# A one-core decoder block: operands of the second feed-forward and of the mixer moved by 128 bytes, and one operand laid out in two regions

## The chip, the cores and the metric

The kernel runs on one core of one Trainium2 chip, as one program. The metric is the device time in microseconds, the median of several runs.

## The reference

The reference is one layer of a decoder block on 256 tokens with 2048 features, preceded by 16 learned tokens (272 rows in all). Everything is float32.

```
hs = concat(meta, x)                                             # 272 x 2048
hs = hs + 0.5 * swiglu(rmsnorm(hs), ffn1_w_gate, ffn1_w_up, ffn1_w_down)   # width 5632
hs = hs + token_mixing(rmsnorm(hs), w_in, ..., w_out)            # two causal convolutions, 3 and 31 taps
hs = hs + 0.5 * swiglu(rmsnorm(hs), ffn2_w_gate, ffn2_w_up, ffn2_w_down)
return rmsnorm(hs)[:, 16:]
```

with `swiglu(h) = (silu(h @ w_gate) * (h @ w_up)) @ w_down`. The weights are read from memory once, 339 MB in all.

## The kernel before, in words

All products are done on TensorE in a split form. Each float32 operand is split into a high part (a rounded copy, `w_hi`, `x_hi`, `a_hi`, `y_hi`, written by ScalarE) and a low part (the difference, `w_lo` and so on, written by VectorE), and a product is the sum of three matmuls: high by high, high by low, low by high. Every matmul has a 128 x 128 stationary operand, which a weight load (LDWEIGHTS, the rows of PEld) puts into the array, and a moving operand that is streamed past it. The load for the next matmul is issued while the current one streams.

The phases follow one another on TensorE in this order: gu1 and down1 (first feed-forward), ag, cv and b (the input projection of the mixer), out_sc and out_cf (its output projection), gu2 and down2 (second feed-forward). Weights come in blocks of 128 x 1024 (512 KB) through a ring of four buffers: a DMA on the SP queue fills `raw`, ScalarE writes `w_hi` from it (L650), VectorE writes `w_lo` (L886), TensorE uses both. ScalarE waits for TensorE to be done with a block four back before it overwrites it.

In gu1, down1, ag, cv, b, out_sc and out_cf the weights are stationary and the activations are moving: 272, 260 or 256 columns, three matmuls a product (`product`, L466 high by high, L467 weight high by activation low, L468 weight low by activation high). In gu2 the weights are stationary too, but high and low activations are streamed in one matmul of 512 columns (`wide_product`, L473), and the third product is a second matmul of 256 columns (L474). In down2 (`last_group`) the roles are swapped: the activations `a2_both` are stationary and the weights are the moving operand, 512 columns (L567, L568, L569).

Where the operands lie is written by hand. The numbers are bytes within a partition. The ring buffers start at a multiple of 512 and each block is 4096 bytes, so a stationary tile of weights (128 columns, 512 bytes) and a moving piece of weights (512 columns, 2048 bytes) start at a multiple of 512. The regions `x_at` and `a_at` start at a multiple of 512 as well. From there, all taken modulo 256:

- gu1 and ag: row tile k of `x_hi` (1088 bytes each) starts at 64 k, that of `x_lo` 64 further.
- down1: `a_hi` at 64 k, `a_lo` 128 further. cv: `x_hi` at 64 k + 48. b: `x_hi` at 64 k + 64.
- out_sc and out_cf: `y_hi` and `y_lo` (1024 bytes a tile, the two parts 16384 bytes apart) all start at 64, since `mix_at` is `a_at + 64`.
- gu2: `x2_both` (2048 bytes a row tile, high part then low part without a gap) always starts at 0.
- down2: the stationary tiles of `a2_both` (512 bytes) start at 0.

`gu2_lo` is a staging buffer that ScalarE fills from PSUM at the end of each gu2 group. `y_f`, `cs`, `zc`, `z`, `zd`, `tap_product` and the `ln_` rows are the mixer's working buffers behind `y_both`; they are placed relative to `mix_at` and are read and written by ScalarE and VectorE.

Of the kernel before, what the change touches and what calls it, by code (L numbers as in the profile page):

```python
# [29 lines left out]
F32R = mybir.dt.float32r  # L30

P = 128
# [4 lines left out]
SET = 4  # L37


def build(nc, x, meta_tokens, ffn1_norm, ffn1_w_gate, ffn1_w_up, ffn1_w_down, mix_norm, w_in, b_in,  # L40
# [3 lines left out]
    SEQ = x.shape[1]  # L44
    META = meta_tokens.shape[0]
    T = META + SEQ
    FF = ffn1_w_gate.shape[2]
    KD = D // P
    KF = FF // P
# [31 lines left out]
    with ExitStack() as ctx:  # L81
# [11 lines left out]
        x_at = nc.sbuf_base  # L93
# [6 lines left out]
        a_at = nc.sbuf_base  # L100
# [18 lines left out]
        def at(name, offset, shape, dt=F32):  # L119
            return nc.alloc_sbuf_tensor_at(name, shape, dt, offset=offset)  # L120

        x_hi = at("x_hi", x_at, [P, KD, T], F32R)
        x_lo = at("x_lo", x_at + 4 * (KD * T + X_GAP), [P, KD, T], F32R)
        x2_both = at("x2_both", x_at, [P, KD, 2, SEQ], F32R)

        o_tok = at("o_tok", x_at, [P, HALVES, D])
        gain_tok = at("gain_tok", x_at + 4 * HALVES * D, [P, D])
        sq_tok = at("sq_tok", x_at + 4 * (HALVES + 1) * D, [P, HALVES, BANK])
        a1_hi = at("a_hi", a_at, [P, KF, T], F32R)
        a1_lo = at("a_lo", a_at + 4 * (KF * T + A_GAP), [P, KF, T], F32R)  # L130
        a2_both = at("a2_both", a_at, [P, 2, KF, SEQ], F32R)
        a_of = {"gu1": (a1_hi, a1_lo),
                "gu2": (a2_both[:, 0, :, :], a2_both[:, 1, :, :])}

        gu2_lo = at("gu2_lo", a_at + 4 * 2 * KF * SEQ, [P, SET, SEQ])
        assert SET * SEQ <= 2 * KF * (T - SEQ)

        x_tok = at("x_tok", a_at, [P, HALVES, D])
        m_rows = at("m_rows", a_at + 4 * HALVES * D, [P, HALVES, P])
# [1 line left out]
        gain_rows = at("gain_rows", a_at + 4 * (HALVES + 1) * D + 16 * P, [KD, P])  # L141

        tile_bytes = 4 * SEQ
        mix_at = a_at + 64
        y_both = at("y_both", mix_at, [P, 2, 2 * KS, SEQ], F32R)
        y_hi, y_lo = y_both[:, 0, :, :], y_both[:, 1, :, :]
        y_f = at("y_f", mix_at + 4 * KS * tile_bytes, [P, KS, SEQ])
# [25 lines left out]
        def param(name, i):  # L173
            if name == "ffn1":
                return gain1[:, i:i + 1]
            return par[:, 0, row0[name] + i:row0[name] + i + 1]
# [55 lines left out]
        def slot(phase, g, i):  # L232
            return (n_blocks[phase] * g + i) % RING if isinstance(g, int) else i % RING
# [7 lines left out]
        def banks_before(phase, g):  # L241

            return KD + SET * group0[phase] + SET * g
# [20 lines left out]
        def over_groups(engine, phase, body):  # L264

            n = n_groups[phase]
            body(0, 0)
            if n > SET:  # L270
                with engine.Fori(1, n - 1, 2) as g:
                    body(g, 1)
                    body(g + 1, 0)
            else:
                for g in range(1, n - 1):
                    body(g, g % 2)
            if n > 1:
                body(n - 1, 1)
# [5 lines left out]
        def tokens(phase):  # L284

            return slice(T - width[phase], T)
# [131 lines left out]
        def _(pe):  # L418
# [13 lines left out]
            def start_between(i):  # L432

                if i in (0, 1, 3):
                    for q in {0: (2, 3), 1: (4, 5), 3: (6, 7)}[i]:
                        turn_pair(q)
                if i == 5:
                    pe.wait_ge(par_loaded, 16 * (len(rows0) + 4))
                    pe.wait_ge(emptied, KD)
                    for s in range(4):  # L440
                        pe.transpose(ps[:, 4, s * P:s * P + n_rows[s]], par_rows[0:n_rows[s], s, :],
                                     ident[0:n_rows[s], 0:n_rows[s]]).then_inc(par_turned, 1)
# [20 lines left out]
            def product(bank, n, w_high, w_low, act_high, act_low, first, last):  # L463

                dst = ps[:, bank, 0:n]
                pe.matmul(dst, w_high, act_high, start=first, stop=False)  # L466
                pe.matmul(dst, w_high, act_low, start=False, stop=False)  # L467
                return pe.matmul(dst, w_low, act_high, start=False, stop=last)  # L468

            def wide_product(bank, w_high, w_low, act_both, act_high, first, last):  # L470

                wide = ps[:, bank, :].rearrange("p (b t) -> p b t", b=2)
                pe.matmul(wide, w_high, act_both, start=first, stop=False)  # L473
                return pe.matmul(ps[:, bank, 0:SEQ], w_low, act_high, start=False, stop=last)  # L474

            def start_group(phase, g):

                if phase != "gu1" or not isinstance(g, int) or g > 0:
                    pe.wait_ge(emptied, banks_before(phase, g) - SET)

            def start_block(phase, g, i):

                pe.wait_ge(lo_ready, before_block(phase, g, i) + 1)

            def square_sums(norm, phase):

                pe.wait_ge(sum_ready[norm], 5 if norm == "start" else KD)
                pe.matmul(ps[:, 7, 0:width[phase]], ones[:, :], sq_sum[:, tokens(phase)],
                          start=True, stop=True).then_inc(stats_done[norm], 1)

            def paired(phase, norm):
                toks = tokens(phase)

                def body(g, parity):
                    first_group = isinstance(g, int) and g == 0
                    start_group(phase, g)
                    if norm and isinstance(g, int) and g == 1:
                        pe.wait_ge(var_ready[norm], 1)
                        if norm == "start":
                            pe.wait_ge(par_ready, 4)  # L500
                    for i in range(n_blocks[phase]):
                        s = slot(phase, g, i)
                        opening = norm == "start" and first_group
                        if opening and i == 0:
                            pe.wait_ge(first_lo, 1)
                        else:
                            start_block(phase, g, i)

                        for j, c in ([(j, c) for c in range(4) for j in range(2)] if opening
                                     else [(j, c) for j in range(2) for c in range(4)]):  # L510
                                k = 4 * (i // 2) + c
                                if norm and first_group and i % 2 == 0 and j == 0:
                                    pe.wait_ge(xlo_ready[norm], k + 1)
                                if opening and i == 0 and c == 2 and j == 0:
                                    start_block(phase, g, i)
                                cols = slice(c * 256 + j * P, c * 256 + (j + 1) * P)
                                bank = SET * parity + 2 * (i % 2) + j
                                if phase == "gu2":
                                    m = wide_product(bank, w_hi[s][:, cols], w_lo[s][:, cols],
                                                     x2_both[:, k, :, :], x2_both[:, k, 0, :],  # L520
                                                     k == 0, k == KD - 1)
                                else:
                                    m = product(bank, width[phase], w_hi[s][:, cols], w_lo[s][:, cols],
                                                x_hi[:, k, toks], x_lo[:, k, toks], k == 0, k == KD - 1)
                        m.then_inc(block_used, 1)
                        if norm and first_group and i == (6 if norm == "start" else 3):
                            square_sums(norm, phase)
                        if norm == "start" and first_group:
                            start_between(i)
                over_groups(pe, phase, body)  # L530

            def single_group(phase, g, parity, high, low, first_k, toks, n_k, ready, per_block, extra=None):
# [108 lines left out]
        def _(act):  # L641
# [10 lines left out]
            def operand(phase, norm, t):  # L652

                toks = tokens(phase)

                act.wait_ge(emptied, 2 * (t // 2) + 2 if norm == "start" else banks_before(norm, 0) + t + 1)
                dst = x2_both[:, t, 0, :] if phase == "gu2" else x_hi[:, t, toks]
                act.activation(dst, res[:, t, toks], ACT.Copy,
                               scale=param(gain_of[norm], t)).then_inc(xhi_ready[norm], 1)

# [219 lines left out]
        def _(dve):  # L880
# [8 lines left out]
            def operand(phase, norm, t):  # L889

                toks = tokens(phase)
                dve.wait_ge(xhi_ready[norm], t + 1)
                high, low_part = ((x2_both[:, t, b, :] if phase == "gu2" else (x_hi, x_lo)[b][:, t, toks])
                                  for b in (0, 1))
                dve.scalar_tensor_tensor(low_part, res[:, t, toks], param(gain_of[norm], t),  # L895
                                         high.bitcast(F32), ALU.mult,
                                         ALU.subtract).then_inc(xlo_ready[norm], 1)
# [350 lines left out]
```

## Time and profile before

| | us |
|---|---|
| median of 3 runs | 1882.8 (1873.69, 1882.8, 1882.98) |
| the profiled execution | 1873.64 |
| its span, first to last instruction | 1871.8 |
| TensorE busy | 1859.9 (99%) |
| TensorE weight loads busy | 1758.7 (94%) |
| VectorE busy | 1112.3 (59%) |
| ScalarE busy | 922.3 (49%) |
| mean granted TensorE clock | 0.999 of full speed |

The time lies 1.8 us over the span. A matmul's duration runs from its start to the modelled end of its results, so successive matmuls overlap in the records; how fast TensorE works is read from the distance between the starts of two matmuls. In a stretch of the window view, the count in brackets holds the matmuls that overlap the stretch, so the two or so that began before it are counted too.

### The profile page before, as it was taken

The numbers are of one execution on the slowest core, as the hardware profiler recorded it, in microseconds if no ns is written. First come the engines' busy times: TensorE is split into PE (matmuls) and PEld (weight loads), VectorE is DVE, ScalarE is ACT, GpSimd is POOL, SyncE is SP. The second block draws the span as 40 slices with busy tenths as digits, with TensorE's granted clock in tenths as the row PEclk, the third lists the DMA queues.
The fourth block names the chain that finished last, engine by engine and source line by source line (L and its number), as shares of the span: only waits on it lengthen the run. The fifth ranks groups of instructions, "written<-read, shape, count | busy, mean of one in ns | idle before, by whom it ended". The sixth has DMA issues, their size and how long they took to land.

```text
span 1871.8 us, 32101 instructions
## 1 busy us (share of the span) xinstructions
PE 1859.9 (99%) x13017; PEld 1758.7 (94%) x13017; DVE 1112.3 (59%) x1218; ACT 922.3 (49%) x1173; POOL 5.9 (0%) x17
## 2 busy tenths in 40 slices
PE   9999999999999999999999999999999999999998
PEld 9999999999999999999999999888888888888886
DVE  7555555555554545468899887555566655544444
ACT  6434333343343444359888665444444444443443
POOL 1000000000000000000000000000000000000000
PEclk9999999999999999999999999999999999999999
DMA  6655555555555555555666566666656666666664
GB/s 222 192 178 173 175 178 170 178 174 173 179 172 178 176 175 178 176 174 170 187 185 178 173 201 186 189 189 189 190 179 188 191 192 193 210 193 190 193 190 134
DMA packets 283357, 342.26 MB, mean 183 GB/s; under 512 B 10639, under 2 KB 223985, under 8 KB 283152
## 3 DMA queue, kind: packets, MB, share of 16 engines
q1 hardware_dynamic: 282672, 340.44, 58.6%
q8 instruction: 57, 0.93, 0.2%
q10 hardware_dynamic: 320, 0.53, 0.1%
q14 instruction: 20, 0.16, 0.0%
q0 software_dynamic: 288, 0.19, 0.0%
HBM read 339.02 MB, written 2.10 MB: 182 GB/s over the span
## 4 chain that ended last, share of the span: by engine, by line
PE 98%; DVE 1%; DMA 0%; ACT 0%; SPq 0%; issue 0%; DVEq 0%
PE ps L466 20%; PE ps L467 20%; PE ps L468 20%; PE ps L473 17%; PE ps L474 9%; PE ps L568 4%; PE ps L567 4%; PE ps L569 4%; DMA x_tok<-in_x 0%; DVE w_lo L886 0%; PE ps L428 0%; PE ps L585 0%; DVE zc L1098 0%; PE ps L591 0%; DVE ln_mu L912 0%; SPq L323 0%
## 5 line engine op out<-in xcount | busy, mean ns | idle before, releaser
L886 DVE TENSOR_TENSOR w_lo<-raw,w_hi 128x1024 fp32r<-128x1024 f32 x639 | 781.7, 1224 | 652.5 <-ACT w_hi L650 647.4
L650 ACT ACTIVATE w_hi<-raw 128x1024 fp32r<-128x1024 f32 x639 | 675.5, 1058 | 845.6 <-PE ps L468 505.6
L466 PE MATMUL ps<-x_hi,w_hi 128*128 128x272 f32 (+2 forms) x2048 | 588.1, 287 | 1.2 <-DVE x_lo L895 1.2
L467 PE MATMUL ps<-x_lo,w_hi 128*128 128x272 f32 (+2 forms) x2048 | 587.3, 287 | 0.0
L468 PE MATMUL ps<-x_hi,w_lo 128*128 128x272 f32 (+2 forms) x2048 | 583.4, 285 | 0.0
L473 PE MATMUL ps<-x_both,w_hi 128*128 128x512 f32 x1408 | 488.4, 391 | 0.0
L474 PE MATMUL ps<-x_both,w_lo 128*128 128x256 f32 x1408 | 394.1, 280 | 0.0
L467 PEld LDWEIGHTS ps<-x_lo,w_hi 128*128 128x128 f32 x2048 | 386.4, 189 | 0.1
L466 PEld LDWEIGHTS ps<-x_hi,w_hi 128*128 128x128 f32 x2048 | 384.5, 188 | 1.5 <-DVE w_lo L1120 1.4
L468 PEld LDWEIGHTS ps<-x_hi,w_lo 128*128 128x128 f32 x2048 | 385.4, 188 | 0.0
L473 PEld LDWEIGHTS ps<-x_both,w_hi 128*128 128x128 f32 x1408 | 263.3, 187 | 57.8
L474 PEld LDWEIGHTS ps<-x_both,w_lo 128*128 128x128 f32 x1408 | 266.1, 189 | 0.0
L467 PE MATMUL ps<-a_lo,w_hi 128*128 128x272 f32 x704 | 202.4, 287 | 0.0
L468 PE MATMUL ps<-a_hi,w_lo 128*128 128x272 f32 x704 | 202.2, 287 | 0.0
L466 PE MATMUL ps<-a_hi,w_hi 128*128 128x272 f32 x704 | 201.9, 287 | 0.0
L567 PE MATMUL ps<-w_hi,a_both 128*128 128x512 f32 x352 | 137.3, 390 | 0.0
L569 PE MATMUL ps<-w_lo,a_both 128*128 128x512 f32 x352 | 137.0, 389 | 0.0
L568 PE MATMUL ps<-w_hi,a_both 128*128 128x512 f32 x352 | 137.0, 389 | 0.0
L468 PEld LDWEIGHTS ps<-a_hi,w_lo 128*128 128x128 f32 x704 | 132.7, 189 | 0.0
L467 PEld LDWEIGHTS ps<-a_lo,w_hi 128*128 128x128 f32 x704 | 132.4, 188 | 0.0
L466 PEld LDWEIGHTS ps<-a_hi,w_hi 128*128 128x128 f32 x704 | 132.4, 188 | 0.0
L765 ACT ACTIVATE tap_product<-z,par 128x256 f32<-128x256 f32 x232 | 98.8, 495 | 0.0
(148 smaller groups left out, 1146.5 us busy)
## 6 DMA issues: line engine op xcount, KB each, us to landing
raw<-in_ffn_w_up SPq DMA_DIRECT2D x176, 512.0 KB, 3.6
raw<-in_ffn_w_down SPq DMA_DIRECT2D x176, 512.0 KB, 4.6
raw<-in_ffn_w_gate SPq DMA_DIRECT2D x175, 512.0 KB, 3.7
raw<-in_w_in SPq DMA_DIRECT2D x80, 512.0 KB, 3.5
raw<-in_w_out SPq DMA_DIRECT2D x32, 512.0 KB, 4.7
x_tok<-in_x SPq DMA_DIRECT2D x4, 512.0 KB, 7.9
gain_tok<-in_final_norm SPq DMA_DIRECT2D x1, 1024.0 KB, 5.3
out_y<-o_tok SPq DMA_DIRECT2D x2, 512.0 KB, 2.9
```

Of the source, the lines that this page charges most:

```text
L466: pe.matmul(dst, w_high, act_high, start=first, stop=False)
L467: pe.matmul(dst, w_high, act_low, start=False, stop=False)
L468: return pe.matmul(dst, w_low, act_high, start=False, stop=last)
L473: pe.matmul(wide, w_high, act_both, start=first, stop=False)
L474: return pe.matmul(ps[:, bank, 0:SEQ], w_low, act_high, start=False, stop=last)
L567: pe.matmul(dst, a_hi[:, k, toks], w_high, start=k == 0, stop=False)
L568: pe.matmul(dst, a_lo[:, k, toks], w_high, start=False, stop=False)
L569: m = pe.matmul(dst, a_hi[:, k, toks], w_low, start=False, stop=k == KF - 1)
L650: act.activation(w_hi[s][:, :], raw[s][:, :], ACT.Copy).then_inc(hi_ready, 1)
L765: act.activation(tap_product[:, q % PRODUCTS, c % 2, :], z[:, c, 2 + n:2 + n + SEQ], ACT.Copy, scale=cf_tap(2 + n, c)).then_inc(cf_product, 1)
L886: dve.tensor_tensor(w_lo[s][:, :], raw[s][:, :], w_hi[s][:, :].bitcast(F32), ALU.subtract).then_inc(lo_ready, 1)
```

## The change

Three groups of addresses change; no instruction is added, removed or moved, and each engine's program is the same list of operations before and after.

- `x2_both`, the moving operand of gu2, starts 128 bytes further, and its layout changes from [row tile][high or low][256] to [high or low][row tile][256]. The 512 moving columns of L473 are then two pieces of 1024 bytes, 16384 bytes apart, in place of 2048 bytes in one piece. Both pieces start at 128 modulo 256.
- `a2_both`, the stationary operand of down2, starts 128 bytes further; `gu2_lo` behind it moves along.
- `mix_at` is `a_at + 192` in place of `a_at + 64`, so `y_both` and all of the mixer's working buffers move by 128 bytes. The moving tiles of out_sc and out_cf then start at 192 modulo 256.

```diff
-        x2_both = at("x2_both", x_at, [P, KD, 2, SEQ], F32R)
+        x2_both = at("x2_both", x_at + 128, [P, 2, KD, SEQ], F32R)
...
-        a2_both = at("a2_both", a_at, [P, 2, KF, SEQ], F32R)
+        a2_both = at("a2_both", a_at + 128, [P, 2, KF, SEQ], F32R)
...
-        gu2_lo = at("gu2_lo", a_at + 4 * 2 * KF * SEQ, [P, SET, SEQ])
-        assert SET * SEQ <= 2 * KF * (T - SEQ)
+        gu2_lo = at("gu2_lo", a_at + 128 + 4 * 2 * KF * SEQ, [P, SET, SEQ])
+        assert 32 + SET * SEQ <= 2 * KF * (T - SEQ)
...
-        mix_at = a_at + 64
+        mix_at = a_at + 192
...
                                     m = wide_product(bank, w_hi[s][:, cols], w_lo[s][:, cols],
-                                                     x2_both[:, k, :, :], x2_both[:, k, 0, :],
+                                                     x2_both[:, :, k, :], x2_both[:, 0, k, :],
                                                      k == 0, k == KD - 1)
...
-                dst = x2_both[:, t, 0, :] if phase == "gu2" else x_hi[:, t, toks]
+                dst = x2_both[:, 0, t, :] if phase == "gu2" else x_hi[:, t, toks]
...
-                high, low_part = ((x2_both[:, t, b, :] if phase == "gu2" else (x_hi, x_lo)[b][:, t, toks])
+                high, low_part = ((x2_both[:, b, t, :] if phase == "gu2" else (x_hi, x_lo)[b][:, t, toks])
                                   for b in (0, 1))
```

## Rows read from the trace of the kernel before

**Rows 1.** The page: busy time of each engine, granted clock, and the chain's shares.

```profile
PE 1859.9 (99%) x13017; PEld 1758.7 (94%) x13017; DVE 1112.3 (59%) x1218; ACT 922.3 (49%) x1173; POOL 5.9 (0%) x17
...
PE 98%; DVE 1%; DMA 0%; ACT 0%; SPq 0%; issue 0%; DVEq 0%
```

**Rows 2.** The page's groups of gu2 and down2: count, busy us, mean ns.

```profile
L473 PE MATMUL ps<-x_both,w_hi 128*128 128x512 f32 x1408 | 488.4, 391 | 0.0
L474 PE MATMUL ps<-x_both,w_lo 128*128 128x256 f32 x1408 | 394.1, 280 | 0.0
...
L567 PE MATMUL ps<-w_hi,a_both 128*128 128x512 f32 x352 | 137.3, 390 | 0.0
```

**Rows 3.** Windows of gu1, down1, cv, out_cf, gu2: busy us (count) by engine, PEclk, DMA.

```profile
100.00:500.00 400.00, 400.00 (x3202) 400.00 (x3201) 206.46 (x202) 159.52 (x167) 0.00 (x0) 1.00 0.56 175
560.00:800.00 240.00, 240.00 (x1927) 240.00 (x1926) 111.27 (x116) 93.68 (x105) 0.00 (x0) 1.00 0.58 176
905.00:960.00 55.00, 55.00 (x465) 55.00 (x465) 49.42 (x69) 47.38 (x88) 0.00 (x0) 1.00 0.59 182
...
1090.00:1120.00 30.00, 30.00 (x257) 30.00 (x256) 23.19 (x38) 17.32 (x27) 0.00 (x0) 1.00 0.67 215
1145.00:1600.00 455.00, 455.00 (x2627) 401.17 (x2626) 273.00 (x250) 217.19 (x228) 0.00 (x0) 1.00 0.61 189
```

**Rows 4.** Timeline of TensorE in down2: start us, duration us.

```profile
1679.66 0.39 PE L569 MATMUL ps<-w_lo,a_both 128*128 128x512 f32 x1
...
1681.70 0.39 PE L569 MATMUL ps<-w_lo,a_both 128*128 128x512 f32 x1
```

**Rows 5.** Timeline in gu2: matmuls, and in the second piece the weight loads.

```profile
1200.31 0.39 PE L473 MATMUL ps<-x_both,w_hi 128*128 128x512 f32 x1
1200.54 0.28 PE L474 MATMUL ps<-x_both,w_lo 128*128 128x256 f32 x1
1200.65 0.39 PE L473 MATMUL ps<-x_both,w_hi 128*128 128x512 f32 x1
...
1200.31 0.19 PEld L474 LDWEIGHTS ps<-x_both,w_lo 128*128 128x128 f32 x1
1200.54 0.19 PEld L473 LDWEIGHTS ps<-x_both,w_hi 128*128 128x128 f32 x1
```

**Rows 6.** Timeline of TensorE in gu1 over one period of four row tiles.

```profile
300.04 0.29 PE L466 MATMUL ps<-x_hi,w_hi 128*128 128x272 f32 x1
300.17 0.29 PE L467 MATMUL ps<-x_lo,w_hi 128*128 128x272 f32 x1
...
300.42 0.29 PE L466 MATMUL ps<-x_hi,w_hi 128*128 128x272 f32 x1
...
300.67 0.28 PE L468 MATMUL ps<-x_hi,w_lo 128*128 128x272 f32 x1
300.79 0.29 PE L466 MATMUL ps<-x_hi,w_hi 128*128 128x272 f32 x1
...
301.17 0.29 PE L466 MATMUL ps<-x_hi,w_hi 128*128 128x272 f32 x1
...
301.54 0.29 PE L466 MATMUL ps<-x_hi,w_hi 128*128 128x272 f32 x1
```

**Rows 7.** The chain of work: the first matmul of gu1.

```profile
10.46 0.36 PE ps L466
```

**Rows 8.** Waits between 1145 and 1600 us (gu2).

```profile
ACT w_hi L650 <- PE ps L474: 182.8, 123, 2.2
DVE w_lo L886 <- ACT w_hi L650: 127.2, 83, 1.7
```

## The prediction

> **What bounds the kernel now.** I read the page first. TensorE is busy 99% of the span and carries 98% of the chain that ended last; VectorE is at 59%, ScalarE at 49% [rows 1]. In gu2 and down2 no group of matmuls has idle time before it [rows 2]. The windows say the same of each phase: 455 us of busy TensorE in 455 us of gu2, at a granted clock of 1.00, that is the upper level, 2.4 GHz [rows 3]. The waits in gu2 run the other way: ScalarE waits 182.8 us for TensorE to give a weight block back and VectorE waits 127.2 us behind ScalarE [rows 8]. So the only thing that can move the time is how fast TensorE gets from one matmul to the next, and a faster TensorE meets engines that now wait for it.
>
> The distance between starts is then the quantity to read. I take the count in a window, subtract the two matmuls that began before it, and divide.
>
> - gu2: 455 / (2627 - 2) = 173.3 ns a matmul, 346.7 ns for a pair of L473 and L474 [rows 3]. 768 columns at 2.4 GHz are 320.0 ns, so a pair carries 26.7 ns beyond its columns, 13.3 ns a matmul.
> - down2: nine matmuls from 1679.66 to 1681.70, 226.7 ns each [rows 4]; 512 columns are 213.3, so 13.3 ns beyond.
> - out_cf: 30 / (257 - 2) = 117.6 ns for 256 columns (106.7), so 11.0 ns beyond [rows 3].
> - gu1: 400 / 3200 = 125.0 ns for 272 columns (113.3), so 11.7 ns. down1: 240 / 1925 = 124.7, so 11.3 ns. cv: 55 / 463 = 118.8 for 260 columns (108.3), so 10.5 ns [rows 3].
>
> This extra is what the change can act on. Over gu2 it is 1408 x 26.7 ns = 37.6 us, over down2 3 x 352 = 1056 matmuls x 13.3 ns = 14.1 us [rows 2], 51.7 us together.
>
> **Does the extra depend on addresses?** Two comparisons say yes. The two phases where both the moving and the stationary operand start at 0 modulo 256 (gu2 and down2) have the largest extra, 13.3 ns, and have it to the nanosecond in both, though one streams activations and the other weights. The phase whose moving tiles always start at 64 (out_cf) has 11.0. And in gu1, where the start of the row tile walks through 0, 64, 128, 192, the step from one matmul to the next is not constant: three matmuls take 0.38, 0.37, 0.38, 0.37 us in turn, and a single one takes from 0.12 to 0.13 [rows 6]. Counted from the first matmul of the phase [rows 7], with each matmul in the trace, the piece shown begins with a row tile at 128; then come 192, 0 and 64. So tiles at 128 and 0 are the slow ones (I read 0.377 us on the mean of the phase, 12.3 ns beyond the columns for each matmul) and those at 64 and 192 the quick ones (0.373 us, 11.0 ns). The cheapest single step shown is L468 with its tile at 192, from 300.67 to 300.79 us, about 7 ns beyond 113.3; the dearest, L466 at 128, from 300.04 to 300.17, about 15 ns beyond at the resolution of the row [rows 6]. The weight load for the next matmul starts within 10 ns of the start of the current one and lasts 0.19 us [rows 5], so it reads its 512 bytes while the moving operand is read, with a fixed relation of the two addresses. My reading: the two reads get in each other's way, and how much depends on that relation.
>
> The Trainium skill, "TensorE: Matmul & The Clock Gate", section "Step-by-step: what each phase is for", says the opposite: TensorE has two independent read ports, and loading the next tile's weights takes no read bandwidth from the running matmul. By that rule this change would be worth nothing. The trace does not agree with it as far as the walk in gu1 goes. The same page's back-to-back gap of N / 2.4 + 2.5 ns would give 215.8 ns for 512 columns; the trace has 226.7, and the trace decides.
>
> **The change part by part.** No instruction is added or moved, so the costs are all in the distance between matmuls.
>
> 1. gu2, moving tiles from 0 to 128. No phase holds this relation all the time. The nearest row is out_cf: a constant start that is not 0, and high and low parts 16384 bytes apart, as the new layout has them. At its 11.0 ns, a pair has 22.0 in place of 26.7: 1408 x 4.7 ns = 6.6 us less. From the walk in gu1, tiles at 128 stand at 12.3 ns: 2816 x 1.0 = 2.8 us less. The bounds are the cheapest and the dearest step of gu1: 7 ns gives 2816 x 6.3 = 17.7 us less, 15 ns gives 4.8 us more. I take 11.0 ns.
> 2. gu2, the 512 columns in two pieces. It costs something only if TensorE does not run over the break. Nothing in this trace streams two pieces in one matmul on this path, so it is bounded by 0 and by the extra of one matmul start, 11.0 ns x 1408 = 15.5 us more. I take 0: the second piece starts at the same place modulo 256 at which the first ends.
> 3. down2, stationary tiles from 0 to 128, moving at 0. The same relation as in 1 with the sign turned. At 11.0 ns: 1056 x 2.3 = 2.4 us less; bounds 1056 x 6.3 = 6.7 us less and 1.8 us more.
> 4. out_sc and out_cf, from 64 to 192. In gu1 tiles at 64 and 192 cost the same (0.37 us for three) [rows 6]. 768 matmuls x 0; bound 1 ns either way, 0.8 us.
> 5. ScalarE and VectorE write and read the same shapes at other addresses. They are at 60% and 48% in gu2 (273 and 217 of 455 us) and wait for TensorE [rows 3, 8], so nothing is taken; a VectorE instruction would have to become about two thirds longer before it showed.
>
> Sum: 6.6 + 2.4 = 9.0 us less. Against the profiled execution that is 1873.6 - 9.0 = 1864.6 us. The median of the runs shown is 9.2 us above it, with one of three runs at the lower value, so the same step from the median gives 1873.8. I forecast 1873.5.
>
> What is faster next? The DMA moves 189 GB/s in gu2 and reached 215 in out_cf [rows 3]; gu2 faster by 1.4% asks for 192. The cover holds.
>
> **The rivals.**
>
> - A. The mild gain above: the relation 128 is one of several that lie between 10.5 and 12.3 ns on the mean, as all other phases do. 13.3 is the highest mean of any phase, and only the phases at 0 have it. For 10.5 to 12.3 ns: 3872 x (2.8 to 1.0) = 10.8 to 3.9 us less, 1872 to 1879. Chance 0.42.
> - B. The strong gain: at a constant relation TensorE settles in a state as cheap as the cheapest step of gu1, since nothing then walks it out again. At 7 to 9.5 ns: 3872 x (6.3 to 3.8) = 24.4 to 14.7 us less, 1858 to 1868. For it: gu2 and down2 are settled states too (each pair equal to the next), only at the dear end. Against it: out_cf is settled and at 11.0. Chance 0.26.
> - C. Nothing: 128 is for this purpose the same as 0. For it: in gu1 the tiles at 128 are as slow as those at 0. Then 1880 to 1885. The skill's rule of independent ports ends here too. Chance 0.21.
> - D. Slower: the break in the middle of each 512 column matmul costs like the start of a matmul. At 11.0 ns it is 15.5 us more, and with the 9.0 less of the rest the time is 1889. It decides from 9.0 us / 1408 = 6.4 ns a matmul on. For it: the moving read jumps by 16384 bytes in mid stream, which no matmul here does. Against it: from one matmul to the next TensorE jumps each time as well, among them jumps of 16384 bytes in out_cf, at 11.0 ns with the weight change and all. Chance 0.11.
>
> **How the numbers follow.** A measurement of this kernel tells about 0.5%, 9.4 us, from no change, and the runs of the kernel before alone lie 9.3 us apart. Case A straddles that line: I put 0.18 of its 0.42 on faster and 0.24 on the same. B is faster, 0.26. C is the same, 0.21. D is slower by 0.10 with 0.01 within. Faster 0.44, the same 0.46, slower 0.10. The range must take in A, the lower part of C and most of B: 1861 to 1884 leaves out D, the fast end of B and the high end of C, 2 in 10. The likeliest case alone has 1872 to 1879.
>
> **What would show it.** In gu2, the distance from L473 to the next L473: 342.0 ns in case A, under 339 in B, 346.7 in C, over 353 in D. In down2 the distance: 224.3, under 223, 226.7. By these two the parts come apart: if gu2 does not move and down2 does, the two regions or the 128 of the moving side is at fault. out_cf should stay at 117.6. I am wrong if the extra comes from something that no address touches, such as the switch of weights itself, or if the settled state at 128 is a dear one, which the 15 ns step of gu1 allows.

## The result, and the profile after

The changed kernel takes 1883.3 us (median of 20 runs, 1883.06 to 1885.57). Measured beside it, the kernel before takes 1873.7 us in the median of 20 runs, 12 of them at 1873.3 to 1873.8 and 8 at 1882.6 to 1883.0. The ratio of the changed kernel to the kernel before is 1.0036, with a 95% interval of 1.0024 to 1.0048. The change makes the kernel slower: by 9.8 us against the lower kind of run, and by 0.5 us against the upper kind, so the ratio is a mean over both. What the two kinds are came out of an experiment below (e12). The three runs from which the prediction took its 1882.8 held two of the upper kind.

The two profiled executions can be compared phase by phase: the kernel before, in a run of the lower kind, was profiled at 1873.64 us, with a span of 1871.8, and the changed one has a span of 1881.7, 9.9 us more. The page after says that the bound is the same, TensorE, and that the time is in the matmuls of gu2 and down2. These are the lines that answer to [rows 1, 2]:

```profile
PE 1869.7 (99%) x13017; PEld 1760.0 (94%) x13017; DVE 1111.2 (59%) x1218; ACT 922.0 (49%) x1173; POOL 5.9 (0%) x17
...
L473 PE MATMUL ps<-x_both,w_hi 128*128 128x512 f32 x1408 | 494.6, 394 | 0.0
L474 PE MATMUL ps<-x_both,w_lo 128*128 128x256 f32 x1408 | 398.5, 283 | 0.0
...
L567 PE MATMUL ps<-w_hi,a_both 128*128 128x512 f32 x352 | 139.3, 396 | 0.0
```

The mean durations grew by 3, 3 and 6 ns, with the same counts and no idle time before them. The windows of the changed kernel (busy us and count by engine) give the distance between starts, as in [rows 3]:

```profile
1090.00:1120.00 30.00, 30.00 (x267) 30.00 (x266) 24.18 (x41) 18.27 (x31) 0.00 (x0) 1.00 0.71 222
1145.00:1600.00 455.00, 455.00 (x2594) 398.88 (x2593) 271.21 (x248) 213.91 (x225) 0.00 (x0) 1.00 0.60 187
```

In gu2 there are 2594 matmuls in the stretch that held 2627 before: 455 / 2592 = 175.5 ns each, 351.1 ns a pair in place of 346.7. In out_cf it is the other way, 267 in place of 257: 30 / 265 = 113.2 ns in place of 117.6. The timeline in down2 (start us, duration us) has eight matmuls from the first row to the last:

```profile
1679.94 0.39 PE L569 MATMUL ps<-w_lo,a_both 128*128 128x512 f32 x1
...
1681.80 0.39 PE L568 MATMUL ps<-w_hi,a_both 128*128 128x512 f32 x1
```

1.86 us / 8 = 232.5 ns, where [rows 4] have 226.7. The granted clock is 1.00 as before and each engine ran the same number of instructions; only the pace of the matmuls changed, and only in the four phases whose operands moved.

From here on a phase's time is the distance from the start of its first matmul to that of the next phase's first; for down2, the last one, it is the distance from the start of its first matmul to that of its last. The changed kernel's gu2 begins and ends at these rows of its timeline:

```profile
1128.75 0.40 PE L473 MATMUL ps<-x_both,w_hi 128*128 128x512 f32 x1
...
1623.54 0.39 PE L567 MATMUL ps<-w_hi,a_both 128*128 128x512 f32 x1
```

| phase | before | changed | difference, us |
|---|---|---|---|
| gu1, down1, ag, cv, b | 1028.3 | 1028.3 | 0.0 |
| out_sc | 47.2 | 46.5 | -0.7 |
| out_cf | 45.2 | 43.5 | -1.7 |
| gu2 | 488.6 | 494.8 | +6.2 |
| down2 | 243.7 | 249.8 | +6.1 |

The sum is the 9.9 us of the span. "Extra" below is what a matmul takes beyond its columns at 2.4 GHz.

### The profile page after: what moved, and what is told of

It is laid out like the page before. It is cut to its first block, busy times and chain, and to the rows that moved or that the text cites. A ratio compares the mean times of both kernels' runs of the same rounds, so it can differ in the third digit from the quotient of the medians.

```text
span 1881.7 us, 32101 instructions
## 1 busy us (share of the span) xinstructions
PE 1869.7 (99%) x13017; PEld 1760.0 (94%) x13017; DVE 1111.2 (59%) x1218; ACT 922.0 (49%) x1173; POOL 5.9 (0%) x17
## 4 chain that ended last, share of the span: by engine, by line
PE 98%; DVE 1%; DMA 0%; ACT 0%; SPq 0%; issue 0%; DVEq 0%
PE ps L467 20%; PE ps L466 20%; PE ps L468 19%; PE ps L473 17%; PE ps L474 9%; PE ps L569 4%; PE ps L568 4%; PE ps L567 4%; DMA x_tok<-in_x 0%; DVE w_lo L886 0%; PE ps L428 0%; PE ps L585 0%; DVE zc L1098 0%; PE ps L591 0%; DVE ln_mu L912 0%; SPq L323 0%
## 5 line engine op out<-in xcount | busy, mean ns | idle before, releaser
L473 PE MATMUL ps<-x_both,w_hi 128*128 128x512 f32 x1408 | 494.6, 394 | 0.0
L474 PE MATMUL ps<-x_both,w_lo 128*128 128x256 f32 x1408 | 398.5, 283 | 0.0
L473 PEld LDWEIGHTS ps<-x_both,w_hi 128*128 128x128 f32 x1408 | 264.5, 188 | 60.9
L567 PE MATMUL ps<-w_hi,a_both 128*128 128x512 f32 x352 | 139.3, 396 | 0.0
L568 PE MATMUL ps<-w_hi,a_both 128*128 128x512 f32 x352 | 139.0, 395 | 0.0
```

Source lines behind the costliest of these rows:

```text
L567: pe.matmul(dst, a_hi[:, k, toks], w_high, start=k == 0, stop=False)
L568: pe.matmul(dst, a_lo[:, k, toks], w_high, start=False, stop=False)
```

## The experiments

**e1_two_regions: the split alone.**

```diff
-        x2_both = at("x2_both", x_at, [P, KD, 2, SEQ], F32R)
+        x2_both = at("x2_both", x_at, [P, 2, KD, SEQ], F32R)
```

The three uses are indexed accordingly.

> The kernel before with one part of the change: the moving operand of gu2 in two regions, still starting at 0 modulo 256. Theory P (position: the extra time of a matmul is set by where its two operands start relative to each other modulo 256, the split costs nothing): gu2 lasts 488.6 us as before, the whole 1873.5. Rival S (split: the break in the middle of the 512 columns costs time): gu2 lasts about 494.8 us as in the changed kernel, 4.4 ns more for each L473, the whole 1879.7.

Measured: 1873.5 us, ratio 1.0001 (0.9991 to 1.0010), gu2 488.6 us. The window from 1145 to 1600 us has the count of the kernel before:

```profile
1145.00:1600.00 455.00, 455.00 (x2627) 401.18 (x2626) 272.94 (x250) 217.20 (x228) 0.00 (x0) 1.00 0.61 189
```

Two pieces 16384 bytes apart cost nothing against one. Rival S falls.

**e2_gu2_shift: the 128 bytes of gu2 alone, in one region.**

```diff
-        x2_both = at("x2_both", x_at, [P, KD, 2, SEQ], F32R)
+        x2_both = at("x2_both", x_at + 128, [P, KD, 2, SEQ], F32R)
```

> The kernel before with one part of the change: the moving operand of gu2 in one region as before, but 128 bytes further. Theory P: gu2 lasts 494.8 us as in the changed kernel (351.1 ns a pair), the whole 1879.7. Rival S: 488.6 us as before (346.7 ns a pair), the whole 1873.5.

Measured: 1879.7 us, ratio 1.0033 (1.0021 to 1.0046), gu2 494.8 us, all other phases unchanged. The count is that of the changed kernel:

```profile
1145.00:1600.00 455.00, 455.00 (x2594) 398.77 (x2593) 271.24 (x248) 213.99 (x225) 0.00 (x0) 1.00 0.60 187
```

So all 6.2 us of gu2 are the start position of its moving operand.

**e3_a2_shift: the 128 bytes of down2 alone.**

```diff
-        a2_both = at("a2_both", a_at, [P, 2, KF, SEQ], F32R)
+        a2_both = at("a2_both", a_at + 128, [P, 2, KF, SEQ], F32R)
```

`gu2_lo` moves along.

> The kernel before with one part of the change: the stationary operand of down2 128 bytes further. Theory P: down2 lasts 249.8 us in place of 243.7, 5.8 ns more a matmul, the whole 1879.6. Rival N (down2 is slower in the changed kernel by what gu2 or the mixer leaves behind): 243.7 us as before, the whole 1873.5.

Measured: 1879.6 us, ratio 1.0033 (1.0020 to 1.0045), down2 249.8 us. Rival N falls. The profiled execution also held something that I had not expected: out_cf took 43.5 us with the mixer still at 64, and this execution took 1877.9 us where the other five took 1879.4 to 1880.0. Windows of out_cf, gu2 and down2:

```profile
1090.00:1120.00 30.00, 30.00 (x267) 30.00 (x266) 24.29 (x42) 18.49 (x30) 0.00 (x0) 1.00 0.69 223
1145.00:1600.00 455.00, 455.00 (x2627) 397.92 (x2626) 274.41 (x250) 215.96 (x228) 0.00 (x0) 1.00 0.61 189
1657.00:1707.00 50.00, 50.00 (x217) 40.54 (x216) 24.27 (x23) 20.32 (x22) 0.00 (x0) 1.00 0.59 183
```

out_cf has 267 matmuls in 30 us at the same addresses at which [rows 3] have 257: one position can have more than one pace. Three single times of the kernel before, 1871.7 to 1872.0 among some 80 near 1873.5, fit that.

The beginning of gu2 in the same profile says when a pace changes. These are the 3rd and 23rd pair of gu2, then the 45th and 65th, in the timeline (start us, duration us):

```profile
1130.63 0.40 PE L473 MATMUL ps<-x_both,w_hi 128*128 128x512 f32 x1
...
1137.70 0.40 PE L473 MATMUL ps<-x_both,w_hi 128*128 128x512 f32 x1
...
1145.82 0.39 PE L473 MATMUL ps<-x_both,w_hi 128*128 128x512 f32 x1
...
1152.75 0.39 PE L473 MATMUL ps<-x_both,w_hi 128*128 128x512 f32 x1
```

Twenty pairs take 7.07 us and then 6.93 us, 353.5 and 346.5 ns a pair, at the same addresses. Between them, after the 32nd pair, TensorE does the one other product of this phase, the sum of squares (L488, at 1140.53 us). The step is 353.5 up to it and, after a short wait behind it, 346.7 to the end of the phase. So a pace belongs to an unbroken stream of matmuls, and a foreign matmul or a wait in between can change it.

**e5_ring_shift: the changed kernel with the ring of weights 128 bytes further as well.**

```diff
-        sb("to_w", [P, (-nc.sbuf_base % (4 * P)) // 32 * 8])
+        sb("to_w", [P, (-nc.sbuf_base % (4 * P)) // 32 * 8 + 32])
```

> The changed kernel, with the ring of weight buffers 128 bytes further too, so that the relation of the moving to the stationary operand modulo 256 is that of the kernel before in gu2, down2 and the two output phases, while their own positions stay those of the changed kernel. Theory P (only the relation counts): gu2 488.6, down2 243.7, out_sc and out_cf together 92.4 us, the whole about 1873.5, if gu1 and the rest keep their time. Rival A (the own position of the activation operand counts): 494.8, 249.8 and 90.0 us, the whole 1883.3.

The pad lies ahead of the ring, so the buffers behind the ring move along with it.

Measured: 1873.1 us, ratio 0.9998 (0.9988 to 1.0008), gu2 488.8, down2 243.7, out_cf 45.2 us. out_sc took 46.5 us as in the changed kernel, where Theory P needed 47.2. Windows of out_cf, gu2 and down2:

```profile
1090.00:1120.00 30.00, 30.00 (x257) 30.00 (x256) 23.07 (x38) 17.32 (x28) 0.00 (x0) 1.00 0.66 217
1145.00:1600.00 455.00, 455.00 (x2627) 397.89 (x2626) 273.01 (x249) 216.92 (x228) 0.00 (x0) 1.00 0.61 189
1657.00:1707.00 50.00, 50.00 (x222) 41.39 (x222) 25.46 (x23) 20.31 (x23) 0.00 (x0) 1.00 0.61 190
```

Everything that the change had moved is still at its new place, and the paces of the kernel before are back in gu2, down2 and out_cf. For this step of 128 bytes, what counts is where the moving and the stationary operand start relative to each other, not where either lies. Rival A falls. gu1, whose activations nobody moved, says the same. Behind a row tile at 128 the three steps are 127.6, 122.4 and 126.8 ns in the kernel before (means over gu1 without its first group). In e5 they are 127.5, 122.5 and 126.8 ns behind a row tile at 0, which now has that relation to the weights. out_sc does not decide it, since it changes its pace on the way, as the next run shows.

**e4_mix192: the mixer's part alone.**

```diff
-        mix_at = a_at + 64
+        mix_at = a_at + 192
```

> The kernel before with one part of the change: the mixer's buffers at 192 in place of 64. Theory P: out_sc and out_cf together 90.0 us in place of 92.4 as in the changed kernel, all other phases as before, the whole 1871.1. Rival T (out_sc and out_cf have two settled states at one and the same address, and which one they fall into hangs on how they begin, since with only down2's operand moved out_cf already took 43.5 in place of 45.2 us): either 92.4 or 90.0 us, whatever the address, the whole 1871.1 to 1873.5.

Measured: 1871.1 us in 8 of 10 runs and 1882.1 in the other two; ratio 1.0000 (0.9984 to 1.0017) over both kinds, so by that number alone undecided. The profile has out_sc 46.5 and out_cf 43.5, gu2 and down2 as before. In every kernel profiled with the mixer at 192 and the ring in its place out_cf took 43.5 us. At 64 it took 43.5 once (e3) and otherwise went at the pace of 45.2. But out_sc has both paces at 192 too. Its windows in the changed kernel, before and after the layer norm's sum at 1057.9 us (L608, the foreign matmul here), and the second of them in e16, a run described further down:

```profile
1040.00:1055.00 15.00, 15.00 (x135) 15.00 (x134) 14.51 (x23) 12.45 (x24) 0.00 (x0) 1.00 0.44 139
1060.00:1068.00 8.00, 8.00 (x70) 8.00 (x69) 8.00 (x8) 4.63 (x4) 0.00 (x0) 1.00 0.67 219
```

```profile
1060.00:1068.00 8.00, 8.00 (x73) 8.00 (x72) 8.00 (x8) 5.04 (x5) 0.00 (x0) 1.00 0.70 219
```

133 matmuls in 15 us are 113 ns each, 68 in 8 us are 118 ns. Both theories have a part: 64 and 192 each have both paces, and the position seems to shift how often each comes. With the mixer at 192 the runs of the lower kind were at 1870.9 to 1871.4 (e4, e13 and e14, 31 of 32), while the kernel before had only three times at 1872 or less among some 80.

**e6, e7, e8, e9, e10, e11: other positions.** Each kernel is the one before with three numbers changed, shown here for e6; each phase's time is read by itself.

```diff
-        x2_both = at("x2_both", x_at, [P, KD, 2, SEQ], F32R)
+        x2_both = at("x2_both", x_at + 64, [P, KD, 2, SEQ], F32R)
...
-        a2_both = at("a2_both", a_at, [P, 2, KF, SEQ], F32R)
+        a2_both = at("a2_both", a_at + 64, [P, 2, KF, SEQ], F32R)
...
-        mix_at = a_at + 64
+        mix_at = a_at + 128
```

> The kernel before (one region) with the moving operand of gu2 and the stationary one of down2 64 bytes further, and the mixer's buffers at 128. Theory P, with the walk of gu1 as its scale (tiles at 64 and 192 quick, at 0 and 128 slow): gu2 about 482 us (11.0 ns beyond the columns a matmul), down2 about 241.4, the output phases slower than at 64, 93 or more, the whole about 1865. Rival M (the extra only grows with the distance from 0): gu2 about 491.7, down2 about 246.8, the whole about 1880.

> The same with both operands of the second feed-forward 192 bytes further and the mixer's buffers at 0. Theory P with the scale of gu1: gu2 about 482, down2 about 241.4 us, the output phases (now at relation 0, 13.3 ns beyond the columns) 94 us. Rival M: gu2 about 497.9, down2 about 252.8 us if it grows on, 491.7 and 246.8 if it is symmetric about 128.

> The same with both operands of the second feed-forward 32 bytes further and the mixer's buffers at 32, to see how fine the position works. Theory P with steps of 64 bytes: gu2 between its values at 0 (488.6) and 64. Rival G (only whole steps of 64 bytes count): gu2 488.6 and down2 243.7 us as before.

> The kernel before with the moving operand of gu2 and the stationary one of down2 96 bytes further and the mixer's buffers at 160. So far gu2 takes 488.6 us at 0 and 32, 497.8 at 64, 494.8 at 128, 497.9 at 192; down2 243.7 at 0, 250.6 at 32 and 64, 249.8 at 128, 245.9 at 192; the output phases together 93.9 at 0, 91.9 at 32, 92.4 at 64, 93.6 at 128, 90.0 at 192. Theory P, read as a smooth curve between these: gu2 about 496, down2 about 250, the output phases 91 to 92 us. Rival Z (each position has a settled state of its own, with no order between neighbours): any of the three outside these.

> The same with both operands of the second feed-forward 160 bytes further and the mixer's buffers at 224. Smooth curve: gu2 about 496, down2 about 248, the output phases 90 to 93.9 us, about 92. Rival Z: outside.

> The same with both operands 224 bytes further and the mixer's buffers at 96. Smooth curve: gu2 between 488.6 and 497.9, about 493, down2 between 243.7 and 245.9, about 245, the output phases about 93 us. Rival Z: outside.

Measured, phase times in us from one profile each; the last column is the median of the whole, whose mixer position is a different one in each row (before 64, e8 32, e6 128, e9 160, changed 192, e10 224, e7 0, e11 96). In gu2 and out_cf it is the moving operand that lies further, in down2 the stationary one, so the relation in down2 has the other sign:

| bytes further | gu2 | down2 | out_cf with the mixer there | whole kernel |
|---|---|---|---|---|
| 0 | 488.6 | 243.7 | 46.1 | 1873.5 (before) |
| 32 | 488.6 | 250.6 | 44.8 | 1879.9 (e8) |
| 64 | 497.8 | 250.6 | 45.2 | 1890.2 (e6) |
| 96 | 493.2 | 251.6 | 46.1 | 1886.0 (e9) |
| 128 | 494.8 | 249.8 | 46.1 | 1883.3 (changed) |
| 160 | 488.5 | 250.6 | 45.6 | 1880.9 (e10) |
| 192 | 497.9 | 245.9 | 43.5 | 1886.6 (e7) |
| 224 | 497.9 | 250.5 | 45.4 | 1891.2 (e11) |

The runs of each kernel in the rows from 32 on agree within 1 us (the changed one has a single run 2 us above), so the one profile stands for them. No expectation that set an order between positions held in gu2 and down2 together, though single numbers came true: Rival M's 497.9 us for gu2 at 192, Rival G's 488.6 for gu2 at 32, and the 94 us of the output phases at 0. gu2 at 64 and 192, which gu1 had as quick places, is the slowest of all, with 224; 160 is as good as 0 between two bad neighbours; 32 does nothing to gu2 and costs down2 6.9 us. Rival Z (no order between neighbours) is what stands. The window of gu2 at 64; at 160 it has the 2627 matmuls of position 0:

```profile
1145.00:1600.00 455.00, 455.00 (x2578) 396.37 (x2577) 270.25 (x247) 212.65 (x224) 0.00 (x0) 1.00 0.60 186
```

Position 0 is the best of eight for down2 and shares the best for gu2, in the profiles kept. Before the change both were at the best place of the eight.

**e12_late_gu2: the kernel before, gu2 begun under another timing.**

```diff
                     start_group(phase, g)
+                    (phase == "gu2" and first_group and
+                     [pe.matmul(ps[:, 0, 0:P], ones[:, :], ones[:, :], start=True, stop=True) for _ in range(3)])
```

> The kernel before with three small matmuls of 128 columns put ahead of gu2, whose result is overwritten, so that gu2 begins under another timing. The kernel before falls in some executions about 9.3 us behind, in 8 of 20 beside the changed kernel and in none of 23 or 14 in later calls. 9.3 us are 6.6 ns for each of 1408 pairs in gu2, which is the distance from 346.7 to 353.3 ns that gu2 shows at 64 and 192. Theory B (gu2 has two settled states at position 0, and its beginning decides): gu2 488.6 or 497.9 us, and times of both kinds over the executions. Rival E (the 9.3 us come from somewhere else, such as the start of the program): gu2 488.6 us always; a slow profile shows the time in another phase.

Measured: 1883.5 us in 10 of 12 runs and 1874.1 in the other two, where the kernel before beside it had 17 runs at 1873.3 to 1873.9 and 14 at 1882.7 to 1883.1. The profile fell into the upper kind; gu2 takes 498.0 us, down2 243.7. Its window of gu2, at position 0:

```profile
1145.00:1600.00 455.00, 455.00 (x2577) 394.58 (x2576) 270.14 (x247) 213.11 (x224) 0.00 (x0) 1.00 0.61 185
```

2575 starts in 455 us are 353.4 ns a pair at the very addresses at which [rows 3] have 346.7. The first part of Theory B holds: gu2 at position 0 has two settled paces, 9.4 us apart over the phase. Its second part, that the beginning decides, does not hold as it stands. In this profile gu2 starts at 353.5 ns a pair and goes on at 353.3 after the sum of squares; e3 and e5 start at 353.5 too and change to 346.7 there. So it is the restart after that sum that set the pace of the rest. What draws the pace there is not known. The three matmuls went with a share of 10 of 12 upper runs against 14 of 31 beside them, which is thin for 12 runs, and the kernel before alone had 8 of 20, 0 of 23, 0 of 14, 14 of 31 and 9 of 23 in its sets of runs. That the upper runs of the kernel before are this same state is inferred from the equal 9.3 us, since none of them was profiled. out_cf took 45.8 us here at its usual pace (257 matmuls in 30 us); the rest is the three added matmuls, and with them each kind of run is 0.6 us later than without.

**e15_half_load: half the stationary tile in gu2.**

```diff
-                                cols = slice(c * 256 + j * P, c * 256 + (j + 1) * P)
+                                cols = slice(c * 256 + j * P, c * 256 + (j + 1) * P - (P // 2 if phase == "gu2" and 0 < k < KD - 1 else 0))
```

The destination is the first 64 partitions for these tiles.

> The kernel before, with a stationary tile of 64 in place of 128 columns in gu2 for all row tiles but the first and the last of each group, the moving operand untouched; it leaves out half of the products of gu2 there. Theory P (the extra is the read of the next stationary tile meeting the moving read): with half the bytes to read, the extra of 26.7 ns a pair falls to about half, 13 ns, and gu2 to about 472 us. Rival F (a fixed price for changing the stationary tile, whose size depends on position): 346.7 ns a pair and 488.6 us as before.

Measured, in the one execution taken (1867.5 us): gu2 482.1 us, between the two theories. In the timeline the half tiles follow one another so:

```profile
1299.91 0.39 PE L473 MATMUL ps<-x_both,w_hi 128*64 128x512 f32 x1
...
1300.25 0.39 PE L473 MATMUL ps<-x_both,w_hi 128*64 128x512 f32 x1
...
1300.93 0.39 PE L473 MATMUL ps<-x_both,w_hi 128*64 128x512 f32 x1
```

Three pairs in 1.02 us are 340 ns a pair, an extra of 20 in place of 26.7 ns. The size of the load matters here, by a quarter of the extra where half was expected.

**e16_half_out192 and e17_half_out0: the same in the output phases, at 192 and at 0.**

```diff
-                dst = ps[:, bank, 0:n]
+                dst = ps[0:w_high.shape[-1], bank, 0:n]
...
-                            cols = slice(c * 512 + j * P, c * 512 + (j + 1) * P)
+                            cols = slice(c * 512 + j * P, c * 512 + (j + 1) * P - (P // 2 if phase in ("out_sc", "out_cf") and 0 < k < n_k - 1 else 0))
```

> The kernel before with the mixer's buffers at 192 and, in out_sc and out_cf, a stationary tile of 64 in place of 128 columns for all row tiles but the first and the last of a group; it leaves out half of those products. Theory F2 (a fixed part of about 6.7 ns a matmul, and a part from the two reads on top): at 192 the extra is already 6.7, so out_cf stays at 43.5 us. Theory P alone (all of the extra comes from the read of the stationary tile): the extra falls to about 4 ns a matmul, out_cf to about 42.4 us.

> The same with the mixer's buffers at 0, where the extra is 13.3 ns with full tiles (out_cf 46.1 us in the runs at 0 and 128). Theory F2: the part above 6.7 ns is halved for the 6 of 8 row tiles with half a load, so about 10.8 ns on the mean and out_cf about 45.1 us. Theory P alone: 8.3 ns, out_cf about 44.2 us. If the size of the load does nothing, 46.1.

Measured, in one execution each (1870.6 and 1872.0 us): out_cf 43.5 us at 192, as with the full tile, and 44.2 at 0 in place of 46.1. Windows of out_cf, e16 and then e17:

```profile
1090.00:1120.00 30.00, 30.00 (x267) 30.00 (x266) 24.25 (x41) 18.65 (x32) 0.00 (x0) 1.00 0.70 224
```

```profile
1090.00:1120.00 30.00, 30.00 (x263) 30.00 (x261) 23.73 (x40) 17.88 (x29) 0.00 (x0) 1.00 0.68 219
```

At 192 half the load changes nothing in out_cf: 113.2 ns for 256 columns, 6.5 to 6.7 beyond them, is a floor that neither position nor the size of the load touches here. At 0, where a full load costs 13.3, the half load brings it to 8.5 on the mean, further down than the 10.8 that I had worked out with a part in proportion, and near the 8.3 of Theory P alone. The timeline says why: among half tiles alone, twelve matmuls take from 1099.89 to 1101.25 us, 113.3 ns each. They stand at the floor, and what is left of the extra is at the full tiles and next to them. So at 0 half the load takes away the whole of the part above the floor. F2 is right about the floor and wrong about the slope. In out_sc the half tile at 192 did gain, 46.0 in place of 46.5 us: it stayed at 113 ns after the layer norm's sum, where the full tile had gone to 118 (the windows of out_sc above).

**e13_mix192_gu160 and e14_mix192_two: versions to beat both.** Both are the kernel before with `mix_at = a_at + 192`; e13 has `x2_both` at `x_at + 160`, e14 has it in two regions at `x_at`.

> The kernel before with the mixer's buffers at 192 and the moving operand of gu2 (one region) at 160, down2 untouched. Theory P (each phase keeps what it showed at its position): gu2 488.5, the output phases 90.0, down2 243.7, the whole 1871.1. Theory B adds: if position 160 has only the quick state, no execution is some 10 us behind, where the kernel before has such ones on this chip. Rival: it has both states, as position 0.

> The kernel before with the mixer's buffers at 192 and the moving operand of gu2 in two regions at position 0. Theory P: 1871.1, gu2 488.6 us. Theory B: executions of both kinds, 1871.1 and 1882, as the two regions change nothing. Rival R (the two regions hold gu2 in the quick state): 1871 in each execution, on a chip on which the kernel before falls into both.

Measured: e13 1871.3 us, ratio 0.9970 (0.9953 to 0.9987), 11 of 12 runs below 1871.5 and one at 1873.7. e14 1871.2 us, ratio 0.9969 (0.9952 to 0.9985), all 12 runs between 1870.9 and 1871.4, while the kernel before had 14 runs near 1873.5 and 9 near 1882.9 on the same chip. In both the output phases take 90.0 us, gu2 488.6 and down2 243.7. The window of out_cf in e14:

```profile
1090.00:1120.00 30.00, 30.00 (x267) 30.00 (x267) 24.19 (x41) 18.52 (x31) 0.00 (x0) 1.00 0.71 223
```

These beat the kernel before by 2.4 us against its lower kind of run and by 11.7 against its upper. Neither showed the upper kind in 12 runs. Whether position 160 or the two regions prevent it, or only shift its odds, is not settled: e4, with one region, had 2 such runs of 10 on a chip on which the kernel before had none of 14.

## Why the prediction was wrong, point by point

- *What bounds the kernel* was right. TensorE has no gap to fill, and all 9.9 us are in its pace. No other engine became the bound: ScalarE still waits 184.8 us for TensorE in gu2, where [rows 8] have 182.8.
- *Does the extra depend on addresses?* Right, and shown by e5 to be the relation of the two operands, though one relation can have two paces. The Trainium skill ("TensorE: Matmul & The Clock Gate", section "Step-by-step: what each phase is for") has it that loading the next tile takes no read bandwidth from the running matmul; these runs speak against that, since at position 0 half a load makes out_cf 1.9 us cheaper (e17 against e7) and at 192 it saves nothing there (e16 against e4). That the two reads collide is the reading that fits; it is argued, since a half tile also writes half as many partitions of PSUM and no row shows a read.
- *Part 1, gu2 from 0 to 128, "I take 11.0 ns"*, is the first step that failed, in its sign. The measured extra is 15.5 ns a matmul: 1408 x (351.1 - 346.7) ns = 6.2 us more in place of 6.6 less, and beyond the 4.8 more that was the dear bound. The reasoning behind it failed as well, in case A: "13.3 is the highest mean of any phase, and only the phases at 0 have it". I took the place at which two phases stood for the bad one because it had the highest number of the few that the trace showed. The other seven positions had gu2 at up to 16.7 (64, 192 and 224), and none below 13.3. The trace held one number for each kind of matmul at a constant position, and comparing gu2 (512 and 256 columns in turn) with out_cf (256 throughout) compared two kinds, not two positions. For out_cf's own kind the guess was right: at 0 it stands at 13.3, among its dearest places (46.1 us at 0, 96 and 128).
- *The walk of gu1*, on which "tiles at 64 and 192 are quick" rests, does not carry over. There each matmul meets its neighbour at another position; at a constant one, gu2 at 64 and 192 is slowest.
- *Part 2, the split, 0*, was right (e1).
- *Part 3, down2, "2.4 us less"*, failed like part 1: 19.2 ns a matmul by the rows above, 6.1 us more. It lies beyond the 15 ns that I had set as the dearest bound, since I took that bound from gu1's single steps. Even with the bounds of parts 1 and 3 at their dear ends the sum had 6.6 us more, where 12.3 were measured, and no case with a chance held it. The last sentence of the prediction named it, "if the settled state at 128 is a dear one", without a chance.
- *Part 4, the mixer, 0 with a bound of 0.8*, had the wrong size: 2.4 us less. It is not the price of an address alone, since e3 had the 1.7 us of out_cf at 64.
- *The base.* 1882.8 was the median of three runs of a kernel with two kinds of run, and the lower kind is the commoner (12 of 20 beside the changed kernel). "The same step from the median" added 9.2 us that belong, as inferred above, to another pace of gu2. Against the profiled execution the forecast was 1864.6, and the changed kernel's profiled execution took 1883.5. That the measured 1883.3 lies within 1861 to 1884 is luck: the range was laid from a base 9.1 us above the 1873.7 that the same kernel showed in 20 runs, and the loss just about filled that gap.
- *The rivals.* D had the right sign and a wrong cause: slower, but not by the break in the 512 columns. C (nothing) had gu1's equal steps at 0 and 128 for it, and those do not speak about a constant position either. No rival with a chance said that 0 may be a good place.

What stays open is the mechanism below "relation": what the two operands collide over, what draws one of two paces after a break, and why neighbours 32 bytes apart differ by 9 us in gu2 and by 7 in down2. No rule that I could form gives the table.

## What to carry to other kernels

Where TensorE runs without gaps, take the distance between starts minus columns over clock as a quantity of its own, for each phase. It hangs on the two operands' relative start and on the pace that the stream fell into after its last break. It can be tried for several phases in one kernel and read from one profile, if the other runs' times say that the profile was a usual one, and it is not to be guessed from a neighbour of another width. Before a median is taken as the base of a sum, look at whether the single runs lie in groups: here a group was, as far as the profiles go, a phase that had settled at another pace, and a change of position moves the paces and seems to move the odds with them.

## What the runs showed of the hardware that I had not expected

- At one and the same set of addresses an unbroken stream of matmuls keeps one of several paces for hundreds of microseconds: gu2 at position 0 with 346.7 or 353.4 ns a pair, out_cf at 64 with 117.6 or 113.2 ns a matmul. In these profiles such a pace changed only where another matmul or a wait broke the stream (gu2 in e3 and e5, out_sc in the changed kernel).
- 32 bytes are enough: down2 goes from 243.7 to 250.6 us.
- 256 columns never went below about 113.2 ns with a new stationary tile each time, 6.5 to 6.7 over the columns, with a full load at 192, with half a load there and with half loads at 0.
